# RWKV preparation fills: low-rank products paired on upper and lower array rows in four banks, six banks in the stage without scan, shift rows stored from a small tile

## The reference, cut to what matters

```python
prev = jnp.concatenate([past_shift.astype(p_shift.dtype), p_shift[:, :-1]], axis=1)
xs = p_shift + (prev - p_shift) * P['rwkv_mu'][l]
r, k, v, wd, ad = _split(xs, RWKV_SIZES)
w_log = -jax.nn.softplus(-(P['rwkv_w0'][l] + jnp.tanh(wd) @ P['rwkv_w_up'][l])) - 0.5
a = jax.nn.sigmoid(P['rwkv_a0'][l] + ad @ P['rwkv_a_up'][l])
...
return y + bonus.reshape(B, T, RWKV_WIDTH), S_fin, p_shift[:, -1:]
```

## Time and profile before

| | us |
|---|---|
| median of three runs | 4704.79 (4702.94 to 4711.39) |
| profiled execution, whole | 4707.36 |
| its span, first to last instruction | 4705.5 |
| mean granted TensorE clock | 0.967 of 2.4 GHz |
| no-scan stage, first layer (TensorE's first matmul to its last z) | 78.72 to 163.68 |
| first scan stage | 222.15 to 325.5 |

### The profile page before, as it was taken

How to read it: one execution, slowest core, us unless ns; L and a number is a source line. 1 busy time by engine, 2 the same in 40 slices (tenths; PEclk the granted TensorE clock), 3 DMA queues, 4 the chain that set the end, 5 groups by cost and what they waited for, 6 DMA issues and landing times. The chain is left out here.

```text
span 4705.5 us, 74875 instructions
## 1 busy us (share of the span) xinstructions
PE 4334.4 (92%) x29488; PEld 3017.3 (64%) x29488; DVE 2280.0 (48%) x4684; ACT 1643.2 (35%) x3886; POOL 814.2 (17%) x980
## 2 busy tenths in 40 slices
PE   7999998989989989999979999989888999899999
PEld 3666665667666667777436666655666566677774
DVE  2556664345524453534425665633455244535344
ACT  4333433445523442211043334333555234421220
POOL 0011010000010015544300110000000100245443
PEclk9999998999999999999989999999999999999999
DMA  5110012010021112222241210120100211123222
GB/s 195 23 35 13 28 25 87 14 36 14 12 87 56 53 65 92 95 102 76 85 192 23 35 15 26 25 88 17 31 16 11 87 58 57 70 88 111 89 72 84
DMA packets 150655, 280.77 MB, mean 60 GB/s; under 512 B 51546, under 2 KB 77402, under 8 KB 145059
## 3 DMA queue, kind: packets, MB, share of 16 engines
q1 hardware_dynamic: 150306, 275.99, 18.3%
HBM read 230.96 MB, written 42.62 MB: 58 GB/s over the span
## 5 line engine op out<-in xcount | busy, mean ns | idle before, releaser
L1054 PE MATMUL banks<-hT,w_piece 128*128 128x384 f32 x1536 | 545.2, 496 | 4.4 <-ACT raw L1159 4.1
L1054 PEld LDWEIGHTS banks<-hT,w_piece 128*128 128x128 f32 x1536 | 279.4, 193 | 171.6 <-issue 11.8
L2233 PE MATMUL banks<-hT,w_piece 128*128 128x384 f32 x1056 | 354.1, 489 | 1.5 <-ACT sb_gate_raw L2343 1.5
L2233 PEld LDWEIGHTS banks<-hT,w_piece 128*128 128x128 f32 x1056 | 196.1, 190 | 141.4 <-issue 16.6
L1999 DVE SCALAR_TENSOR_TENSOR keysT<-banks,gains,rstd 64x128 f32<-64x128 f32 (+1 forms) x272 | 112.1, 412 | 252.9 <-ACT rstd L1913 250.4
L2689 DVE TENSOR_TENSOR gate_quarters<-gate_kept,banks 128x288 f32<-128x288 f32 x144 | 65.4, 454 | 298.4 <-PE banks L2552 293.4
L2640 ACT ACTIVATE gate_kept<-banks 128x288 f32<-128x288 f32 x144 | 59.0, 410 | 431.9 <-PE banks L2552 431.9
L2689 DVE TENSOR_TENSOR branch_quarters<-branch_kept,banks 128x288 f32<-128x288 f32 x144 | 65.4, 454 | 265.0 <-PE banks L2552 264.7
L2405 DVE TENSOR_TENSOR_SCAN left<-pass,zero 128x384 f32<-128x384 f32 (+7 forms) x144 | 190.5, 1323 | 5.0
L2402 DVE TENSOR_TENSOR pass<-pass,constants 128x128 f32<-128x128 f32 x128 | 40.8, 319 | 312.8 <-ACT take L2354 310.2
L1015 POOL TENSOR_TENSOR state_decayed<-state,decay_of_chunk 128x128 f32<-128x128 f32 x120 | 85.9, 716 | 547.4 <-DVE state L1288 547.4
(11 more groups left out here) (425 smaller groups left out, 9801.8 us busy)
## 6 DMA issues: line engine op xcount, KB each, us to landing
w_piece<-in_w_cols SPq DMA_DIRECT2D x66, 512.0 KB, 4.4
w_ada<-in_w_ada SPq DMA_DIRECT2D x24, 1024.0 KB, 9.6
w_gate_ahead<-in_w_cols SPq DMA_DIRECT2D x48, 512.0 KB, 4.3
w_branch<-in_w_br SPq DMA_DIRECT2D x96, 256.0 KB, 2.9
w_gate<-in_w_cols SPq DMA_DIRECT2D x48, 512.0 KB, 4.3
y_branch<-y_gated SPq DMA_DIRECT2D x12, 1152.0 KB, 8.0
sb_cached_keysT<-in_sbkT SPq DMA_DIRECT2D x8, 1024.0 KB, 7.6
sb_cached_values<-in_sbv SPq DMA_DIRECT2D x8, 1024.0 KB, 5.1
```

The costliest lines, as they stand in the source:

```text
L1054: last = mm(dst, w[0 if kind in ("k", "v") else 1][:, k, :], hT[:, k, c], start=(k == 0), stop=(k == KD - 1))
L2233: last = mm(ps[:, bank[n], 0:TG], w_of[wn][:, k, :], hT[:, k, TG * g:TG * g + TG], start=(k == 0), stop=(k == KD - 1))
```

## The change

1. `FILL` begins with lw, la alternating by tile instead of three lw and then three la.
2. Each fill has its own bank, `fill_bank`, and its turn there, `turn_of`. In a scan stage the six low-rank fills take banks 0, 1, 2, 3, 0, 1, k's first tile bank 3, and from then on banks 0 and 1 alternate; in the no-scan stage six banks go round. TensorE waits for lw's second tile to be read before it writes the sample's y into bank 2, and for k's first before chunk 3.
3. VectorE copies the last rows into a small tile, `last_rows` (per kind one element and eight elements per partition), at the start of each `shift`. SyncE stores from there, once that shift is done. ScalarE no longer waits for k's store; the stage waits for all six at its end.
4. The stage without preparation keeps its two banks.

```diff
-FILL = [(kind, g) for kind in ("lw", "la", "k", "r", "ss", "v", "bs", "z") for g in range(NTG)]
+FILL = [(kind, g) for g in range(NTG) for kind in ("lw", "la")] + [(kind, g) for kind in ("k", "r", "ss", "v", "bs", "z") for g in range(NTG)]
...
-        free = (free0, free1)
+        free = (free0, free1, free2, free3, free4, free5)
         fills, chunk_of = (FILL, fill_chunk) if prep else (GATE_FILL, gate_chunk)
+        if not prep:
+            fill_bank = [x % 2 for x in range(len(GATE_FILL))]
+        elif scan:
+            fill_bank = [0, 1, 2, 3, 0, 1, 3] + [x % 2 for x in range(len(FILL) - 7)]
+        else:
+            fill_bank = [x % len(free) for x in range(len(FILL))]
+        turn_of = [fill_bank[:x].count(b) for x, b in enumerate(fill_bank)]
...
+            last_rows = sb("last_rows", [P, 3, 1 + NB])
...
         def released(eng, kind, g):
             n = FILL_AT[kind, g]
-            eng.wait_ge(free[n % 2], n // 2 + 1)
+            eng.wait_ge(free[fill_bank[n]], turn_of[n] + 1)
...
-                for kind in "krv":
-                    released(sp, kind, 2)
-                    done = k_stored if kind == "k" else rv_stored
-                    sp.dma_start(O["shift_p"][l, 4 * mu_of[kind] + nx], raw_of[kind][:, TP - 1:TP]).then_inc(done, 16)
-                    sp.dma_start(O["shift_s"][l, 4 * mu_of[kind] + nx], raw_of[kind][:, TP + TS - 1:T:TS],
-                                 allow_slow_non_contiguous=True).then_inc(done, 16)
+                for x, kind in enumerate("krv"):
+                    j = mu_of[kind]
+                    sp.wait_ge(shifted, x + 1)
+                    sp.dma_start(O["shift_p"][l, 4 * j + nx], last_rows[:, j, 0:1]).then_inc(shift_stored, 16)
+                    sp.dma_start(O["shift_s"][l, 4 * j + nx], last_rows[:, j, 1:]).then_inc(shift_stored, 16)
...
                     if k == 0:
-                        if n >= 2 and prep:
-                            pe.wait_ge(free[n % 2], n // 2)
+                        if prep:
+                            if turn_of[n] >= 1:
+                                pe.wait_ge(free[fill_bank[n]], turn_of[n])
...
             pe.wait_ge(u_added, 1)
+            if prep:
+                released(pe, "lw", 1)
...
                 i, c = divmod(n, 2)
+                if prep and n == 3:
+                    released(pe, "k", 0)
                 pe.wait_ge(s_scaled, n + 2)
...
                     if g == 0:
                         if kind != "k":
                             act.wait_ge(shifted, 1 if kind == "r" else 2)
-                        if kind == "v":
-                            act.wait_ge(k_stored, 32)
...
                 released(dve, kind, 2)
+                V.tensor_copy(last_rows[:, j, 0:1], raw_of[kind][:, TP - 1:TP])
+                V.tensor_copy(last_rows[:, j, 1:], raw_of[kind][:, TP + TS - 1:T:TS])
```

More of the change, by code:

```diff
@@ L911, in rwkv_fused @@
     names = ("w0_loaded", "w1_loaded", "par_done", "fill_ready", "free0", "free1", "summed", "exps_done",
-             "z_sigmoid", "shifted", "squared", "maxed", "rooted", "prod_done", "r_done", "k_stored", "rv_stored",
+             "z_sigmoid", "shifted", "squared", "maxed", "rooted", "prod_done", "r_done", "shift_stored", "free2", "free3", "free4", "free5",
              "state_out", "u_ready", "u_added", "y_ready", "y_copied", "s_ready", "s_scaled",
@@ L915, in rwkv_fused @@
     with S.stage(*names) as (block, sb, (w0_loaded, w1_loaded, par_done, fill_ready, free0, free1, summed, exps_done,
-                                         z_sigmoid, shifted, squared, maxed, rooted, prod_done, r_done, k_stored, rv_stored,
+                                         z_sigmoid, shifted, squared, maxed, rooted, prod_done, r_done, shift_stored, free2, free3, free4, free5,
                                          state_out, u_ready, u_added, y_ready, y_copied, s_ready, s_scaled,
                                          stat_in, stat_out, y_normed, y_turned, y_gated, y_stored, z_gated, sd_made, g_sigmoid, g_made, g_stored, ahead_loaded, ends_stored, vec, act_own)):
-        free = (free0, free1)
+        free = (free0, free1, free2, free3, free4, free5)
         fills, chunk_of = (FILL, fill_chunk) if prep else (GATE_FILL, gate_chunk)
+        if not prep:
[5 more added lines that the diff above has]
+        turn_of = [fill_bank[:x].count(b) for x, b in enumerate(fill_bank)]
         lead, mid, end = (FILL_LEAD, FILL_MID, FILL_END) if prep else (GATE_LEAD, GATE_MID, GATE_END)
@@ L998, in _ @@
             if prep:
-                sp.wait_ge(k_stored, 32)
-                sp.wait_ge(rv_stored, 64)
+                sp.wait_ge(shift_stored, 96)
             if not scan:
@@ L1127, in evacuate @@
                 kind, g = fills[n]
-                c, src = cols(g % NTG), ps[:, n % 2, 0:TG]
+                c, src = cols(g % NTG), ps[:, fill_bank[n], 0:TG]
                 if kind in ("ss",):
@@ L1135, in evacuate @@
                 if kind == "lw":
-                    ACTE.activation(t[0][:, c], src, ACT.Sigmoid, bias=par[:, W0C:W0C + 1]).then_inc(free[n % 2], 1)
+                    ACTE.activation(t[0][:, c], src, ACT.Sigmoid, bias=par[:, W0C:W0C + 1]).then_inc(free[fill_bank[n]], 1)
                 elif kind == "la":
-                    ACTE.activation(aT[:, c], src, ACT.Sigmoid, bias=par[:, A0:A0 + 1]).then_inc(free[n % 2], 1)
+                    ACTE.activation(aT[:, c], src, ACT.Sigmoid, bias=par[:, A0:A0 + 1]).then_inc(free[fill_bank[n]], 1)
                 elif kind == "z":
-                    ACTE.activation(R.zs[nx % 2][:, c], src, ACT.Copy).then_inc(free[n % 2], 1)
+                    ACTE.activation(R.zs[nx % 2][:, c], src, ACT.Copy).then_inc(free[fill_bank[n]], 1)
                 elif kind == "bs":
@@ L1143, in evacuate @@
                         act.wait_ge(r_done, 1)
-                    ACTE.activation(rT[:, c], src, ACT.Copy).then_inc(free[n % 2], 1)
+                    ACTE.activation(rT[:, c], src, ACT.Copy).then_inc(free[fill_bank[n]], 1)
                 else:
@@ L1155, in evacuate @@
                         if s is None:
-                            ACTE.activation(um[:, b], ps[:, n % 2, a], ACT.Copy, scale=mu)
+                            ACTE.activation(um[:, b], ps[:, fill_bank[n], a], ACT.Copy, scale=mu)
                         else:
-                            ACTE.activation(seqs(um[:, b])[:, :, 1:], ps[:, n % 2, a].rearrange("p (b t) -> p b t", t=TS), ACT.Copy, scale=mu)
-                    ACTE.activation(raw_of[kind][:, c], src, ACT.Copy).then_inc(free[n % 2], 1)
+                            ACTE.activation(seqs(um[:, b])[:, :, 1:], ps[:, fill_bank[n], a].rearrange("p (b t) -> p b t", t=TS), ACT.Copy, scale=mu)
+                    ACTE.activation(raw_of[kind][:, c], src, ACT.Copy).then_inc(free[fill_bank[n]], 1)
             ACTE.preload_act_table_set("sigmoid_and_others")
@@ L1304, in _ @@
                             dve.wait_ge(fill_ready, FILL_AT["ss", g] + 1)
-                            own(V.tensor_scalar(t[0][:, cols(g)], ps[:, FILL_AT["ss", g] % 2, 0:TG], 1e-24, None, ALU.max), maxed if g == NTG - 1 else None)
-                            V.engine_nop().then_inc(free[FILL_AT["ss", g] % 2], 1)
+                            own(V.tensor_scalar(t[0][:, cols(g)], ps[:, fill_bank[FILL_AT["ss", g]], 0:TG], 1e-24, None, ALU.max), maxed if g == NTG - 1 else None)
+                            V.engine_nop().then_inc(free[fill_bank[FILL_AT["ss", g]]], 1)
                     if n == 6:
```

2 lines of the change are left out of this document (1 added, 1 removed).

## The result

The changed kernel takes **4653.84 us** in the median of four runs (4652.63 to 4655.26); the kernel before, run beside it, 4708.09 (4702.94 to 4712.83). The ratio is 0.9887, 95% interval 0.9872 to 0.9902: 54 us less, where 21 had been forecast, and outside the range. The profiled execution took 4652.63 us, its span 4650.8, against 4707.36 and 4705.5.

The account below looks back on a forecast made before the run. TensorE, busy 92% of the span, was taken as the bound. First layer 10.30, second 4.33 and scan stages 6.36 sum to 21.0 us, off a median of 4704.79: 4683.8 us, range 4674 to 4693.

Parts of the forecast that it names:

- The start of the no-scan stage: Six low-rank products, 7.70 us, shrink to 4.48; 1.61 us won per layer, or 3.22 if the clock rose earlier.
- the clock moves: Rival: low-clock stretches of 2.7 us shift; three more give 4691.9 us (7%), three fewer at scan-stage joints 4675.7 (7%).
- The v stall: No-scan v products: without ScalarE's wait for k's store v takes 15.48 us, winning 6.72 us (first layer) and 0.75 (second).
- Six banks: No-scan one-matmul fills stop waiting for evacuations: sums of squares win 1.05 us, bonus sums 0.92, in each layer.
- the ring: Two alternating banks of the no-scan stage, said to make TensorE wait for evacuations at the one-matmul fills.
- Pairs: lw and la on opposite row halves overlap, twelve passes in seven slots; rival that they do not: 4689.7 us, 7%.
- Scan stages: In six stages k starts 1.21 us earlier, less 0.15 for copies: 1.06 each, 6.36 us in all.
- The stores do not end the scan stage: Rival said they do: late sample states cost from a 10.2 us landing on, up to 31.8 us, 4715.6 us; 3%.
- The long wait: Rival: the first layer's v wait is that execution's own, so v gains 0.75 us there, not 6.72: 4689.8 us; 6%.
- stall, sums and bonus: No-scan gains in v, sums of squares and bonus sums: 6.72, 1.05, 0.92 us (first layer); 0.75, 1.05, 0.92 (second).
- attentions and merge: Code the change does not touch, after each layer's fused stages; taken as unchanged, 0 us.

Follow-up runs that it names:

- before with the pause of four: Kernel before, with TensorE waiting for four memsets (485 ns each) on VectorE ahead of each layer's latent attention: 4702.61 us, ratio 0.9998 to the kernel before.
- store-alone kernel: Kernel before with only the stores out of last_rows and no wait for k_stored: 4692.26 us against 4699.58, ratio 0.9984.
- The kernel with lw and la one after the other: Changed kernel with low-rank fills in the old order, in two banks in the no-scan stage: 4677.61 us, ratio 0.9948 to the kernel before.

## Why the prediction was wrong

**The start of the no-scan stage: the step that failed first.** The forecast said that nothing in the trace shows the rise of the clock following the amount of work, and took 1.61 us; the other value it named was 3.22. Measured, start to end of r: 41.16 us before (78.72 to 119.88) and 34.59 after (78.14 to 112.73), **6.57**; second layer, 41.24 and 36.06, **5.18**. Even 3.22 was no upper bound. It only let the five slots between twelve and seven be won at half speed, and forgot that an earlier rise also gives k's first passes their full speed (2.40 us in the first layer, beside 4.17 up to k). Over the three and two traces the start to the end of r takes 40.8 and 35.2 us in the first layer and 41.3 and 36.1 in the second, so 5.5 and 5.2 are won on average. The trace of before held a hint: all six 64-row matmuls and the first 5 us of k run at 0.50, although TensorE is busy from 78.72 on. I took the moment of the rise as given and did not ask what it waited for. What the runs showed in its place: with two passes side by side the clock rises 2.9 to 6.2 us after the first pass, in place of 10.1 to 13.1.

**Unchanged code taken as unchanged time: the step that cost most.** "The last fused stage of a layer, and all after it, is unchanged" was true of the code and wrong by 17.1 us in the two profiled executions, of which the 8.4 in layer 2 repeat in all five traces of the two kernels; by the averages it is 12.1. The rival "the clock moves" was the right mechanism with the wrong size and place: it looked at the joints of six scan stages, three stretches of 2.7 us, and not at the 3,100 us behind them, where the traces of before have 22 to 25 low stretches and those of after 18 and 19. The measured size of this effect for one moved start is the step between the two cases of the latent attention, some 8 us.

**The v stall** was right in its mechanism: v takes 130.14 - 114.66 = 15.48 us, to the hundredth, and 15.48 in the second layer, and the low stretch at 137 is gone. Its price was that of one execution. In the five traces of kernels with the old stores v takes 22.2, 19.1, 21.5, 21.4 and 24.7 us in the first layer and 16.2, 16.6, 22.4, 20.0 and 16.1 in the second, so the change wins 3.6 to 9.2 us and 0.6 to 7.0 us, where the forecast had 6.72 and 0.75. The longest idle stood in before with the pause of four:

```profile
137.87 7.88 PE L1054 MATMUL banks<-hT,w_piece 128*128 128x384 f32 x16 [6.37 <-ACT raw L1159]
```

**Six banks** were right: 1.93 and 1.94 us for the one-matmul fills, as summed; the store-alone kernel, which still has the ring, still takes 2.98 and 2.86.

**Pairs** overlap, in six slots and not seven: the first pass of a run has a partner too. The Trainium skill (TensorEngine Tiling (Array Packing), Theoretical Speedup) gives up to 2x, and the trace agrees with it rather than with my reading of the earlier trace rows. The six pairs start at 78.14, 78.91, 79.55, 80.19, 80.83 and 81.23, and the earlier trace rows had shown it too: four passes in 0.85 us are two slots of 0.44.

**Scan stages.** At full clock one went from 103.36 to 101.84, 1.52 us instead of 1.06. k starts 1.75 us earlier, not 1.21: ScalarE evacuates a tile every 0.47 us, where I had 0.65. That 0.65 was read wrongly: before, a tile comes out of TensorE only every two passes of 0.3225 us, and ScalarE waited for it. The kernel with lw and la one after the other shows ScalarE's own pace for three tiles of one kind, starts at 2551.43, 2551.90 and 2552.36:

```profile
2551.43 1.52 ACT L1149 ACTIVATE a_gate<-banks,parameters 128x384 f32<-128x384 f32 x3
```

Of the 1.75 the end of the stage keeps 1.52, so the copies cost at most 0.23; the store-alone kernel has 0.19 (forecast 0.15). Six times 1.52 is 9.1; the other 4.9 of the 14.0 are low stretches. The kernel before begins four of the six stages with one, as here its second (window of the same form as above), and the changed one, at the same joint, with none:

```profile
385.05:388.40 3.35, 3.35 (x8) 1.57 (x9) 0.59 (x5) 2.40 (x2) 0.86 (x1) 0.52 0.01 2
```
```profile
368.90:372.30 3.40, 3.40 (x17) 1.77 (x18) 1.85 (x7) 3.18 (x4) 0.90 (x1) 1.00 0.01 2
```

The changed kernel has one too, at its first scan stage in one trace (103.45 us, 101.85 in the other).

**The other rivals.** The stores do not end the scan stage: the states land in 8.7 us in the median and 9.3 at most, below the 10.2 from which it would have cost anything. They are sent as late as forecast, 91.8 us into the stage. The long wait was not this execution's own in the first layer: TensorE idles 3.3 to 6.4 us in v in all five traces with the old stores. The rival had its point in the second layer, where the idle goes from 0.2 to 4.2 us: 0.75 us was a lucky draw for the kernel before.

**The sum again, with what was measured** between the two profiled executions: the two no-scan starts 11.75 (3.22 forecast); stall, sums and bonus of both layers 11.4 (11.4); scan stages 9.1 (6.4) and their clock 4.9 (0); attentions and merge 17.1 (0); the rest, tails among it, 0.5.

**What stays open:** which moments of a start are good ones. Twenty-six latent attentions have been seen and no rule for them was tested; the pause of four was called wrongly. Nor was it shown why the clock rises earlier in the no-scan stage. That passes on one half of the array alone do not bring it back was not tried apart from the time they take: in all kernels here the side-by-side passes are also the quicker ones.

## What to carry to other kernels

When TensorE is over 90% busy and its mean granted clock is below 1, read where the low stretches lie and what starts them before summing durations: here some 120 of 4,705 us were the clock's, by the estimate above. A matmul of half height leaves the array's other half free, so give the two halves different banks and list them alternately; it paid most where the clock had still to rise (5.5 us at a no-scan start against 1.5 in a scan stage). Take a stall's price from several executions: the one in v cost 3.6 to 9.2 us for the same code. A difference of under 0.3% of such a kernel may be a moved start and no better schedule; the cheap test is a pause of a microsecond ahead of the stage that comes after the edit.

## What the runs showed of the hardware

- Two matmuls on different row halves start in the same instant (78.14 and 78.14) and pass each other in the queue: one listed behind six passes of the other half started about 1.4 us after the first of them.
- The clock rose 10.1 to 13.1 us after the first of the low-rank passes in the 14 starts where they ran one at a time, and 2.9 to 6.2 us after it in the 12 where they ran two at a time.
- The same matmuls behind the same 3.40 us of idle ran at half clock in one execution (6.49 us) and at full clock in another (3.58 us). One and the same latent attention took 526.7 to 530.2 us in 18 cases and 535.7 to 537.1 in eight, and a pause ahead of it moved it from one group to the other.
- A pause of 2.6 us in all made a kernel of 4,706 us 8 us faster (ratio 0.9977 to 0.9996), in the one set of runs that compares the two.
- The store of eight elements per partition lands in 7.8 us in the median out of a small contiguous tile and in 13.7 out of every sixteenth column; the transfer behind it in the queue went from 11.4 to 8.7.
